# Differential attention scores: both banks taken first, the two maps' passes issued in turn

## What is computed

```python
def diff_attention(q, k, v, lam):          # q, k: (B, S, H, 2, 64), already normed; v: (B, S, H, 128)
    ...
        sc = jnp.einsum('bqhmd,bkhmd->bhmqk', q_blk, k).astype(jnp.float32) * scale
        sc = sc - slopes[None, :, None, None, None] * dist
        sc = jnp.where(dist >= 0, sc, NEG_BIG)
        p = jax.nn.softmax(sc, axis=-1)
        a = p[:, :, 0] - lam * p[:, :, 1]
        return jnp.einsum('bhqk,bkhe->bqhe', a.astype(v.dtype), v)
```

## Time and profile before

| | us |
|---|---|
| median of 3 runs | 2038.74 |
| lowest, highest | 2036.72, 2038.78 |
| profiled execution | 2037.95 |
| its span, first to last instruction | 2036.2 |
| TensorE busy in it | 2017.4 (99%) |
| VectorE, ScalarE, GpSimd busy | 1140.5, 888.7, 307.7 |

### The profile page before, as it was taken

How to read it: one execution, slowest core, us unless ns; L and a number is a source line. 1 busy time by engine, 2 the same in 40 slices (tenths; PEclk the granted TensorE clock), 3 DMA queues, 4 the chain that set the end, 5 groups by cost and what they waited for, 6 DMA issues and landing times.

```text
span 2036.2 us, 25187 instructions
## 1 busy us (share of the span) xinstructions
PE 2017.4 (99%) x9832; PEld 1681.0 (83%) x9832; DVE 1140.5 (56%) x2001; ACT 888.7 (44%) x1753; POOL 307.7 (15%) x288
## 2 busy tenths in 40 slices
PE   9999999999999999999999999999999999999997
PEld 6888888888888888878888888788898888888886
DVE  6677884455534444774343345787775664444434
ACT  5454653345423333553222234776654553222224
POOL 2213431011000001331100101222211021110101
PEclk9999999999999999999999999999999999999999
DMA  6222112243333232333322323223342032333222
GB/s 199 83 63 63 52 52 69 88 155 114 94 94 103 93 94 88 92 100 104 103 94 93 103 83 114 68 73 104 100 144 89 27 124 93 95 98 98 95 92 73
DMA packets 62212, 191.54 MB, mean 94 GB/s; under 512 B 6856, under 2 KB 15048, under 8 KB 62092
## 3 DMA queue, kind: packets, MB, share of 16 engines
q1 hardware_dynamic: 62092, 189.93, 29.4%
HBM read 187.69 MB, written 2.21 MB: 93 GB/s over the span
## 4 chain that ended last, share of the span: by engine, by line
PE 94%; DVE 3%; ACT 1%; DMA 1%; SPq 1%; issue 0%; POOL 0%; DVEq 0%; ACTq 0%
PE bank L302 93%; PE bank L307 1%; SPq L171 0%; DMA d_tab<-tab_sb 0%; DMA x_sb<-d_xT 0%; POOL wl L486 0%; DVE wl L486 0%; ACT tmp L180 0%; DVE tmp L186 0%; DVE work L192 0%; ACT h_h L180 0%; DVE pd L186 0%; ACT rsq L180 0%; DVE tmp L183 0%; DVE pd L198 0%
## 5 line engine op out<-in xcount | busy, mean ns | idle before, releaser
L484 ACT ACTIVATE wh<-raw 128x512 fp32r<-128x512 f32 (+1 forms) x696 | 401.2, 609 | 893.3 <-PE bank L302 890.6
L302 PE MATMUL bank<-h_h,wh 128*128 128x512 f32 x1536 | 609.2, 397 | 1.8 <-ACT h_h L180 1.3
L302 PE MATMUL bank<-h_l,wh 128*128 128x512 f32 x1536 | 599.2, 390 | 1.2 <-DVE h_l L186 1.1
L302 PE MATMUL bank<-h_h,wl 128*128 128x512 f32 x1536 | 599.2, 390 | 0.1
L486 DVE TENSOR_TENSOR wl<-raw,wh 128x512 fp32r<-128x512 f32 (+1 forms) x646 | 434.2, 699 | 61.3 <-ACT wh L484 39.6
L302 PEld LDWEIGHTS bank<-h_h,wh 128*128 128x128 f32 x1536 | 288.9, 188 | 66.1 <-issue 4.4
L302 PEld LDWEIGHTS bank<-h_l,wh 128*128 128x128 f32 x1536 | 288.9, 188 | 62.1 <-DVE h_l L186 2.9
L302 PEld LDWEIGHTS bank<-h_h,wl 128*128 128x128 f32 x1536 | 288.6, 188 | 61.4 <-POOL wl L486 0.5
L183 DVE TENSOR_TENSOR tmp<-bank,rstd 128x512 f32<-128x512 f32 x98 | 70.4, 721 | 125.2 <-PE bank L302 124.9
L204 POOL TENSOR_TENSOR tmp<-tmp,rstd 128x512 f32<-128x512 f32 x44 | 63.2, 1438 | 462.6 <-ACT tmp L180 458.8
L486 POOL TENSOR_TENSOR wl<-raw,wh 128x256 fp32r<-128x256 f32 x98 | 80.1, 845 | 305.8 <-ACT wh L484 305.8
(11 more groups left out here) (480 smaller groups left out, 3313.4 us busy)
## 6 DMA issues: line engine op xcount, KB each, us to landing
raw<-d_wts SPq DMA_DIRECT2D x312, 512.0 KB, 3.5
raw<-d_wts SPq DMA_DIRECT2D x24, 384.0 KB, 3.0
x_sb<-d_xT SPq DMA_DIRECT2D x16, 256.0 KB, 5.4
raw<-d_wts SPq DMA_DIRECT2D x28, 128.0 KB, 2.0
d_yT<-x_sb SPq DMA_DIRECT2D x4, 384.0 KB, 3.0
tab<-d_ali SPq DMA_DIRECT2D x4, 256.0 KB, 4.7
tab<-d_dec SPq DMA_DIRECT2D x4, 256.0 KB, 3.5
mraw<-d_memT SPq DMA_DIRECT2D x8, 128.0 KB, 2.3
```

Of the source, the lines that this page charges most:

```text
L302: bank.done = pe.add(lambda e: e.matmul(out, lhsT, rhs, start=first, stop=True, skip_group_check=True), n, w, waits)
L484: p.th = [Op(act, lambda e, c=c: e.activation(H[:, c], raw[:, c], FN.Copy), [p.loads]) for c in (slice(o, min(o + 512, width)) for o in ra ...
```

## The change

The two banks of a block are taken together before the first pass, and then the three kinds of pass are issued for map 0 and map 1 in turn. In the planner, a late 64-row pass is priced at half of what it was.

```diff
@@ b_mm
         if late:
-            n = max(n + 0.0025, 0.055) if lhsT.dtype == F32R else max(4 * n + 0.01, 0.108)
+            n = max(n + 0.0025, 0.055) / (2 if lhsT.shape[0] == 64 else 1) if lhsT.dtype == F32R else max(4 * n + 0.01, 0.108)
@@ differential
             P = yield from grab(pd, 2)
             bs = []
-            for m in range(2):
-                hp = slice(64 * m, 64 * m + 64)
-                b = yield from bank_of(JOB)
-                out = b.ap[:, 0:n]
-                b_mm(b, out, q.h[hp, cs], k.h[hp, 0:n], q.rdy[0], k.rdy[0])
-                b_mm(b, out, q.l[hp, cs], k.h[hp, 0:n], q.rdy[1])
-                last = b_mm(b, out, q.h[hp, cs], k.l[hp, 0:n], k.rdy[1])
-                bs.append(b)
+            bs = yield from grab(JOB, 2)
+            yield [b.free for b in bs]
+            for x, y, tq, tk in ((q.h, k.h, q.rdy[0], k.rdy[0]), (q.l, k.h, q.rdy[1], None), (q.h, k.l, None, k.rdy[1])):
+                for b, hp in zip(bs, (slice(0, 64), slice(64, 128))):
+                    last = b_mm(b, b.ap[:, 0:n], x[hp, cs], y[hp, 0:n], tq, tk)
             spawn(maps(i, P, bs), j)
```

## The result

| | before | after |
|---|---|---|
| median, us (22 runs each) | 2039.7 | 2043.45 |
| lowest, highest | 2036.72, 2041.55 | 2039.52, 2046.14 |
| profiled execution; its span | 2037.95; 2036.2 | 2040.58; 2038.8 |

The ratio is 1.0019, with a 95% interval of 1.0013 to 1.0025: slower by some 3.8 us, where 2.0 us less had been forecast, and above the range's upper end of 2040.8. The profiled executions differ by up to 5.5 us before the edited part is reached, where all kernels are the same; up to 3.4 us of that is TensorE's clock, granted at half for 3.4 to 10.2 us in the first 56 us of a trace. So the traces are compared by distances: from the first differential pass (`qk21h,qk20h`, 512 columns) to the first pass of the mixer's output projection (`mix2d_h,wh`), called **D1**, and to the first score pass of the memory attention (`km_hl,qm0h`), called **D2**. D2 holds the output projection.

A forecast was written before the change was run, and what follows sets the result against it. The prediction took TensorE's passes, one behind the other, to bound the edited stretch. Its terms -1.6 + 0.4 - 1.1 + 0.3, with 0 for the bank pair, gave -2.0 us: 2036.7 us on the median 2038.74, range 2034.2 to 2040.8.

The forecast's parts named there:

- What bounds the kernel: From 1285 to 1474 us TensorE is busy 188.0 of 189.3 us; VectorE, ScalarE and GpSimd have 39, 55, 142 to spare.
- all before it and behind it unchanged: Sign of being right: the stretch to the same memory pass shrinks by some 2 us, the rest of the trace stays.
- The maps run beside each other: Differential score blocks: passes of both maps already run in pairs, so issuing in turn adds 0 for 14 of 16.
- Term 1: Two differential blocks whose maps stand apart (384 and 128 columns): joining each removes its second run, -1.6 us.
- Term 2: Head 0's 512 and 384 blocks: three projection passes now stand between, one more entry and exit, +0.4 us.
- Term 3: Third retention head: TensorE's wait for `str0l` before the second values pass is covered by the new order, -1.1 us.
- Term 4: Retention head 1: its second values pass may wait for low parts on GpSimd behind seven partial sums, +0.3 us.
- Term 5: Taking two of four job banks at once moves rows but adds no semaphore: 0, bound 4.4 us at four differential values passes.
- The waits only move: Rival, 0.20: the 1.1 us return at another head and differential heads add tenths; near 2038.5, up to 2040.8 us.
- GpSimd holds the values: Rival, 0.07: GpSimd's queue falls behind at the four retention heads and TensorE waits; 2043.7 us.
- Strictly in order: Rival, 0.05: paired starts are only drawn, so issuing in turn saves 4.5 us more in adjacent blocks; 2032.2 us.

The follow-up runs named there:

- e2: The kernel before, with only the six passes of each of the 14 adjacent score blocks issued in turn for the two maps: 2038.3 us, ratio 0.9997.
- e9: The kernel before, with the two split differential blocks joined in TensorE's finished queue and no other order changed: 2036.43 us, ratio 0.9990.
- e10: e9 with two VectorE rows swapped, so that the third retention head's `str0l` stands ahead of the first `mem_hl`: 2037.95 us, ratio 0.9995.
- e12: e10 with one more wait on GpSimd: `qk22l` waits until VectorE has done the third retention head's `str0l`: 2036.60 us, ratio 0.9986.
- e3: The changed kernel with the planner's old price for a 64-row pass: 2049.1 us, ratio 1.0050.
- e4: The kernel before with the planner's new price alone, the score code untouched: 2053.16 us, ratio 1.0071.
- e1: The changed kernel with scratch tiles of its own for the last retention head's norm: 2043.7 us, ratio 1.0022.
- e5: The changed kernel with the memory's key norms planned only after the last retention head's root: 2045.01 us, ratio 1.0025.
- e8: The changed kernel run once more, unaltered, for a second time and profile: 2042.81 us, ratio 1.0017 against the kernel before.
- e7: The kernel before with only the planner's price of a late 64-row pass times 1.1: 2047.96 us, ratio 1.0041.

## Why the prediction was wrong, point by point

- **What bounds the kernel.** Right that TensorE alone sets the pace in this stretch; wrong in what it was taken for. 39 us to spare on VectorE are a mean over 189 us. In the 20 us of the memory's keys and values VectorE has 1.9 to spare. And the stretch was cut off at 1474 us because the orders agree again on TensorE from there. ScalarE's and VectorE's had not; they differ as far as the last head's `mix2r_h` and `mix2r_l`. This is **the step that failed**, "all before it and behind it unchanged". What lies behind D1 grew by 2.07 us, of an error of 4.8 us in D2 (+2.76 against -2.0). The other 2.7 us lie in D1, in waits that the sum had at 0 or too small (below).
- **The maps run beside each other; the turn is worth 0.** Right (e2: -0.08 us).
- **Term 1, split blocks, -1.6.** Right in kind, 0.1 too large: 1.48 at the two places (e9), of which 0.88 reached D1.
- **Term 2, lost seam, +0.4.** Right: after, 1284.92 to 1287.43 us less three projection passes of 0.23 is 1.82, against the 1.43 of the earlier trace rows.
- **Term 3, `str0l`, -1.1.** The wait went. Its cause had not been read: the operation ahead of `str0l` on VectorE, one `mem_hl` of 1.54 us, stood beside `qk22l` on GpSimd (e10, e12).
- **Term 4, `str1l` at head 1, +0.3.** Right place and releaser, mis-sized: 0.76. The count was right up to the sums: they start 4.2 us behind head 0's first score pass (1411.83 us) and end 11.0 us behind it, and the second values pass is due at 12.3. What was too small are the two low parts, 1.4 us in the count and 2.04 now:

```profile
1418.27 4.57 POOL L204 TENSOR_TENSOR ssum<-ssum,tmp 128x256 f32<-128x256 f32 x5 [0.58 <-ACT tmp L180]
1422.81 2.04 POOL L204 TENSOR_TENSOR str1l<-tmp,str1h 128x256 fp32r<-128x256 f32 x2
...
1422.68 1.86 DVE L486 TENSOR_TENSOR wl<-raw,wh 128x512 fp32r<-128x512 f32 x2
```

(The merged `str1l` row is the part of 256 columns and that of 128.) VectorE's two panel parts run beside them and are stretched too, 1.86 us instead of 1.29. That the two engines hold each other up here rests on these rows; no run moved them.

- **Term 5, joint request, 0, bound 4 x 1.1.** It was to move rows and add no semaphore. One wait for a bank came, 1.0 us ahead of head 1's values (`std1`, 1345.66), within the bound. By the emitted order these values go to bank 6, which map 0 of head 2's block of 384 columns has held since 1343.5 us. TensorE is released when VectorE's mask pass on that bank ends (the two L198 rows, read until 1346.73); the low part `std1l` ends at 1346.93, too late to be what the first pass waited for, and would have held the second one nearly as long:

```profile
1346.17 0.55 DVE L198 CUSTOM_DVE_ANT_0 pd<-bank,tab 128x384 f32<-128x384 f32 x1
1346.65 0.08 DVE L198 DVE_READ_ACCUMULATOR2_ANT work<- 128x1 f32 x1
1346.65 0.28 DVE L183 TENSOR_TENSOR std1l<-bank,std1h 128x128 fp32r<-128x128 f32 x1
```

Before, 24 passes and not 12 stand between that block and the values. The wait is in neither e3 nor e4, so it belongs to this order and to neither half of the change.

- **Missing terms.** `mem_hl`, 0.86 + 0.53 = 1.4 us, and `mix2r`, 2.04. The sum as measured: -1.48 + 0.4 - 1.1 + 0.76 + 1.0 + 1.4 + 2.04 = 3.0, and some 0.4 less in smaller waits (0.9 now, 1.3 before), so 2.6 against the 2.76 of D2. The step behind a wait is 0.1 us longer as well, which is counted at `mix2r` alone; counted everywhere it adds some 0.3.
- **The rivals.** "The waits only move" (0.20) is what happened, but its upper end of 3.3 us was bounded by the differential heads alone; 5.2 us of new waits came, 1.0 of them there. "GpSimd holds the values" gave nearly the time (2043.7), with the wrong mechanism: one of its four heads waits for GpSimd. "Strictly in order" fell (e2).
- **Range and chances.** With the order new in 190 us of the trace, 0.20 was too little for waits that move, and their bound had to come from every consumer, not from four of them. The range ended 2.65 us below the median measured. It was also narrower than its own terms: with the bound of 4.4 us, and not 3.3, the far end would have been 2041.9, and the low end comes to 2034.4, not 2034.2.

## What to carry to other kernels

Where a change shifts a planned order, its size is the shift, not the edit: rearranging two blocks in the finished queue gave -0.9 us, and the same blocks under a new order +2.8. Follow each engine's order to where it agrees again, not TensorE's alone, and list what stands on a single slot of scratch in between. Where VectorE has little to spare, count GpSimd's work beside it as VectorE's, and the other way round where TensorE waits for GpSimd's result.

## What the runs showed of the hardware

- A VectorE operation that reads two tiles of SBUF can be held until the GpSimd operation beside it ends: `mem_hl` is drawn 1.54 us long beside a `qk22l` of 1.28, 0.47 alone; `str0l` 1.41 and 0.28 (e10, e12). Not every one is: of 18 panel parts of 512 columns (`wl<-raw,wh`) that overlap GpSimd work between 1240 and 1520 us before, ten take their usual 0.68 or 0.69, and the longest 1.8. GpSimd's operations grow as well: `str1l` of 128 columns takes 0.90 us beside VectorE's panel parts after, 0.46 us in the earlier trace rows. Those that read a bank of PSUM are not stretched: `tmp<-bank,rstd` takes 0.68 us at 1437.90 beside GpSimd, and as much alone. The Trainium skill ("SBUF — State Buffer", SBUF: two separate sides) has the two engines share a pair of ports under "an exclusive lock, not a bandwidth split", which whichever starts first holds for the whole instruction, when VectorE has two SBUF inputs; these rows agree.
- The two halves of the array run passes beside each other that stand three apart in the queue: twelve passes take 1.43 us in either order of issue (e2), 2.46 us one at a time by the prediction's count.
- Behind some waits TensorE's clock is granted at half: for 3.4 us at idle times of 2.3 us (e1), 2.9 (e5) and 1.4 (e8), for 10.2 us at one of 5.5 (e3), and in e7 for 3.4 us also behind four idle times of 0.4 to 0.8 us (1446.85 to 1451.74 us). Behind the idle time of 1.2 us at the output projection in the first profile of the change it was not.
